# Two projections with streamed activations: weights queued in front of activations

## Reference

```python
# first block, layer 0 (output projection of the mixer)
y_m = head_rmsnorm(h, mnorm_w) * silu(z)              # 1024 columns
y_p = multiscale_pool(u, pool_w, pool_scale) * silu(z2)  # 1024 columns
y   = concatenate([y_m, y_p], -1) @ w_out             # ab_w_out: 2048 x 1024, 1280 rows
x   = x + gate * rmsnorm(y, g_post)
# first block, layer 1: window attention; then the second block's mixers
...
# second block, feed-forward
h = h + conv_ffn(rms_norm(h, norm_ffn), w_up, conv_w, conv_b, w_down)   # w_down: 2816 x 1024
gate = sigmoid(rms_norm(h, norm_ple) @ w_ple_gate)
h = h + gate * (p @ w_ple_proj)
```

## Time and profile before

| | |
|---|---|
| median of 3 runs | 3276.93 us (3276.76 to 3278.3) |
| the profiled execution, its own time | 3276.24 us |
| its span | 3274.5 us |
| mean granted TensorE clock | 0.992 |
| TensorE matmuls busy | 3194.9 us (98%) |
| VectorE busy | 1918.3 us (59%) |
| ScalarE busy | 1615.8 us (49%) |
| out0's matmuls | about 1092 to 1326 us |
| down's matmuls | about 2892 to 3147 us |

### The profile page before, as it was taken

One profiled execution on the slowest core, in us unless ns is written; L12 is line 12 of the kernel. 1 busy time (PEld: TensorE's weight loads), 2 busy tenths in 40 slices (PEclk: granted clock), 3 DMA queues, 4 the chain that ended last, 5 costly groups with the idle time before them and its releaser, 6 DMA issues. The chain is left out here.

```text
span 3274.5 us, 43387 instructions
## 1 busy us (share of the span) xinstructions
PE 3194.9 (98%) x17352; PEld 2616.6 (80%) x17352; DVE 1918.3 (59%) x2974; ACT 1615.8 (49%) x2603; POOL 113.6 (3%) x246
## 2 busy tenths in 40 slices
PE   7999999999999999999999999998999999999998
PEld 5988889898888887888787778886777888878786
DVE  7554444445345468542688454447669888854555
ACT  5343444435333445314788444416646777743455
POOL 2000000000000000001000000000000000000000
PEclk9999999999999999999999999999999999999999
DMA  5202011120533457203400541110162222255564
GB/s 211 69 5 84 30 56 58 42 72 13 174 102 137 181 204 267 87 26 90 104 2 2 154 131 37 46 37 27 46 206 62 80 82 79 71 180 215 210 224 148
DMA packets 198968, 331.49 MB, mean 101 GB/s; under 512 B 28891, under 2 KB 131392, under 8 KB 198640
## 3 DMA queue, kind: packets, MB, share of 16 engines
q1 hardware_dynamic: 176432, 249.23, 23.2%
q0 software_dynamic: 21264, 79.43, 7.0%
q10 hardware_dynamic: 1072, 0.07, 0.0%
HBM read 281.41 MB, written 47.28 MB: 100 GB/s over the span
## 5 line engine op out<-in xcount | busy, mean ns | idle before, releaser
L413 DVE TENSOR_TENSOR W_rounded<-W,W_rounded 128x2048 fp32r<-128x2048 f32 (+2 forms) x184 | 350.6, 1906 | 408.1 <-ACT W_rounded L404 404.2
L2606 PE MATMUL G<-W_rounded,r_y_rounded 128*128 128x512 f32 x2016 | 472.2, 395 | 7.8 <-DVE W_rounded L413 7.5
L404 ACT ACTIVATE W_rounded<-W 128x2048 fp32r<-128x2048 f32 (+1 forms) x172 | 292.8, 1703 | 350.4 <-DMA W<-in_w_down 61.8
L2606 PEld LDWEIGHTS G<-W_rounded,r_y_rounded 128*128 128x128 f32 x2016 | 378.4, 189 | 95.4 <-DVE W_rounded L413 9.5
L1166 PE MATMUL G<-W_rounded,HT_rounded 128*128 128x512 f32 x640 | 213.7, 415 | 0.0
L2231 PE MATMUL G<-HT_rounded,W_rounded 128*128 128x512 f32 (+1 forms) x768 | 207.8, 355 | 0.0
L1210 PE MATMUL G<-HT_rounded,W_rounded 128*128 128x512 f32 (+1 forms) x768 | 206.6, 355 | 1.0 <-PEq L665 1.0
L2954 PE MATMUL G<-W_rounded,HT_rounded 128*128 128x512 f32 x640 | 201.2, 395 | 0.0
L2231 PEld LDWEIGHTS G<-HT_rounded,W_rounded 128*128 128x128 f32 x768 | 136.6, 188 | 24.8 <-issue 3.5
L1210 PEld LDWEIGHTS G<-HT_rounded,W_rounded 128*128 128x128 f32 x768 | 135.8, 188 | 22.4 <-issue 1.2
L2954 PEld LDWEIGHTS G<-W_rounded,HT_rounded 128*128 128x128 f32 x640 | 118.5, 188 | 28.2 <-issue 2.0
(11 more groups left out here) (544 smaller groups left out, 7074.0 us busy)
## 6 DMA issues: line engine op xcount, KB each, us to landing
W<-in_w_down SPq DMA_DIRECT2D x33, 1024.0 KB, 5.4
W<-in_ab_w_out SPq DMA_DIRECT2D x32, 1024.0 KB, 5.8
up_w_in<-in_w_up SPq DMA_DIRECT2D x44, 512.0 KB, 4.4
W<-in_ab_w_in SPq DMA_DIRECT2D x20, 1024.0 KB, 8.7
W<-in_w_mod SPq DMA_DIRECT2D x8, 2048.0 KB, 8.2
x_rows<-r_xt POOLq DMA_DIRECT2D x32, 512.0 KB, 5.5
W<-in_c_w_out SPq DMA_DIRECT2D x24, 512.0 KB, 6.7
r_xt<-x_rows POOLq DMA_DIRECT2D x24, 512.0 KB, 5.1
```

Source lines behind the costliest of these rows:

```text
L404: ins = a.activation(self.half(key, True)[:, at], self.half(key, False, False)[:, at], ACT.Copy)
L413: ins = v.tensor_tensor(self.half(key, False)[:, at], self.half(key, False, False)[:, at], self.half(key, True)[:, at].bitcast(F32), ALU.s ...
L2606: ins = pe.matmul(slot(r)[:, n * 512:(n + 1) * 512], x[y], w[z][:, k, n * 512:(n + 1) * 512], start=(kk == 0 and k == 0 and (y, z) == SPLI ...
```

## The change

In `rows_part` the load of a step's weights, from the fourth step on, moves from behind the activations' transfer to in front of it, and behind the waits. The condition is the same, so the same items are loaded in the same steps. It holds in the streamed projections alone, which are out0 and down.

```diff
@@ -2564,14 +2564,14 @@
                     prev.room(sp, s)
                 if s < per:
                     prev.arrives(sp, kk)
+                if s >= 3 and K.loaded <= K.pl.items[item]:
+                    K.load_item(sp)
                 sp.dma_start(y_part(s, 0, False), stream[:, 2 * kk:2 * kk + 2, rs[0] * P:(rs[-1] + 1) * P])\
                     .then_inc(s_y[s % 3], 16)
                 if s == 2:
                     prev.left(sp)
                     K.load_item(sp)
                     load_gg()
-                    K.load_item(sp)
-                if s >= 3 and K.loaded <= K.pl.items[item]:
                     K.load_item(sp)
         K.load_phase(sp, key, ahead)
         if tail is not None:
```

## The result

In the first comparison the changed kernel took 3282.57 us (median of 14 runs, 3279.12 to 3285.16) against 3277.11 us (14 runs, 3272.12 to 3282.49): ratio 1.0017, 95% interval 1.001 to 1.0024. In a second one, with the same two programs, the ratio was 1.0008, 0.9999 to 1.0017: there the interval just reaches no change at all. So the change costs some 3 to 5.5 us, less than the 0.2% that the prediction named as what can be told. The forecast of 3279.0 had the sign right and the time inside its range. Its difference, 2.1 us, was too small by more than half of the measured one (5.5) in the first comparison, by about a quarter (of 2.8) in the second.

What follows compares the result with a forecast made beforehand. TensorE's matmuls, busy 98% of the span, were taken to bound the kernel. Three waits at 0.65 us (1.95) and 0 to 0.15 from down's last step gave +2.1 on 3276.93: 3279.0 us, range 3276.2 to 3284.5.

Steps and rivals of the forecast that it cites:

- What bounds, and the untouched start of down: TensorE's matmuls bound, busy 98%; down's longest wait, 3.7 us at its start, has loads issued earlier and is not touched.
- The weights land earlier and nobody uses it: In out0 and down weights land about 0.9 us earlier, unused because ScalarE and VectorE still split the activations first.
- The price of a step, 0.65 us: Activations land 5.92 us after the pair's first issue, their split adds 0.52, so the weights' split starts 0.65 us later.
- The prediction's smaller value, 0.52 a step: If the pair's last byte lands at the same time in either order, only the split's 0.52 is left; sum 1.6.
- Three waits without spare time, 3 × 0.65 = 1.95: Two-tile steps where TensorE already waits, 1.08 and 0.39 us in out0, 2.31 in down, pay in full and add up.
- Rival C: Activations behind the weights meet GpSimd's row traffic and pay 2.57 us more a step: sum 9.7, 3286.6 us; chance 0.13.
- In a step with three tiles nothing: Three-tile steps of out0 and down have 5.8 us to spare, so even 1.0 us later costs TensorE nothing.
- the sign that it had named for being wrong: Wrong if pieces land under 4.5 or over 7 us, TensorE waits in three-tile steps, or many two-tile steps wait.
- The rule on arbitration: DMA engines take turns between queues, so row traffic passes beside the weights and activations run alone; sum stays 2.1.
- The sum on record: Total cost of +2.1 us: 1.95 from three waits in out0 and down, 0 to 0.15 from down's last step.

Runs made afterwards that it cites:

- swap, stores first: Changed kernel with GpSimd's queue in out0 and down reordered, a group's stores before the next group's loads: 3276.36 us, ratio 0.9993 against the kernel before.

## Why the prediction was right, and where it was too small

*What bounds, and the untouched start of down.* Right: the start of down waited 3.9 instead of 3.7 us, in the second profile 3.7. TensorE's longest waits outside the two phases are the same as before within some tenths, but for those in the program's first phase.

*The weights land earlier and nobody uses it.* Right, and the experiments show it from both sides: 4.9 us instead of 5.4, no gain in the changed kernel, 2.6 to 2.8 us by the medians once the splits follow the new order.

*The price of a step, 0.65 us.* The mechanism was right, the size too large. The activations were to land 5.92 us after the first issue; in the last step ScalarE started on them at 5.82, over the last five steps of down at 5.6 by the median. The distance of the two splits was 0.54 for 0.52. The weights' split started at 6.36 for 6.44 in the last step, so it paid 0.34 where the text had 0.4 for it. Over the last five steps the median is 6.12 against 5.75 before, 0.37 us a step. So the pair is complete after 5.6 to 5.8 us in either order, and what is paid is the split of the activations less a small gain. The prediction's smaller value, 0.52 a step, was nearer; the Trainium skill, DMA: Bandwidth & Descriptors, section Anatomy of one DMA, from which it has the rule for that value, gives it for transfers issued by GpSimd, and these two are SyncE's.

*Three waits without spare time, 3 × 0.65 = 1.95.* This is the first term that was mis-sized. Down's grew by 0.4 to 0.5. Out0's second wait, 0.39, vanished. The change need not be the reason: in the second profile of the kernel before it is missing too, and with the swap in out0 only there is one of 0.5 behind the 3.4. Out0's first grew by 1.7 and not 0.65. That waits for L413 grew by 1.9 in all (with 0.2 at the start of down) where the sum had 2.1 is luck: none of the three came out at 0.65. In its step the weights' split started 10.46 us after the first issue (1249.33 to 1259.79), before 8.78 (1247.78 to 1256.56), in the step of the first wait of the earlier trace rows. The first two microseconds after the issue, in the changed kernel and before:

```profile
1249.30:1251.30 2.00, 2.00 (x10) 1.62 (x9) 1.97 (x3) 1.50 (x2) 0.93 (x2) 1.00 0.17 39
```

```profile
1247.80:1249.80 2.00, 2.00 (x10) 1.63 (x9) 1.97 (x3) 1.48 (x1) 0.52 (x1) 1.00 0.57 143
```

39 GB/s against 143: GpSimd's load was issued 0.15 us ahead of the pair (1249.18) where it had been 0.5 ahead (1247.26), so less of it had moved when the pair came. An estimate from these rows: 104 GB/s less over 2 us are 208 KB, at the 408 GB/s of the earlier trace rows 0.5 us. With the 0.54 of the split that explains about 1.0 of the 1.68 us; the rest is open. Rival C had named the clash with the rows' traffic, but as activations that pay for it a second time; what these rows show is a later start for all. The lead of GpSimd's load alone doesn't fix the wait: it was 2.2 us with a lead of 0.28 and the old order in all of out0 (swap in down only), and 2.0 with the old order in this step and a lead of 1.0 (swap with three tiles only). It was also 2.3 us with a single transfer of GpSimd's beside the pair (swap, stores first).

*"In a step with three tiles nothing."* This step of the prediction failed, and the sign that it had named for being wrong, a wait of TensorE in steps with three tiles, is there. It counted the spare time of the weights' split, which was enough (5.8 us), and not who else waits on ScalarE: at the end of a group the squares of the second and third finished row stand behind the two splits, and TensorE needs the row's bank. ScalarE behind the splits of out0's tenth step, before and after:

```profile
1158.76 1.01 ACT L2639 ACTIVATE r_sq<-G 128x1024 f32<-128x1024 f32 x1
```

```profile
1160.14 1.01 ACT L2639 ACTIVATE r_sq<-G 128x1024 f32<-128x1024 f32 x1
```

1.4 us later in all, of which 0.5 is a shift that the steps had already, and TensorE waited 0.92 for `r_ty` where it had waited 0.34:

```profile
1163.81 6.57 PE L2606 MATMUL G<-W_rounded,r_y_rounded 128*128 128x512 f32 x27 [0.92 <-DVE r_ty L2694]
```

With the second such wait, 0.42 us near 1234 that wasn't there before, that makes 1.0 us. The version with the swap in three tiles only has the first at 1.0 and no second.

*The clock.* A term that was missing: the wait in out0 had a price beyond its own length, 1.3 us.

*The rule on arbitration.* The Trainium skill, DMA: Bandwidth & Descriptors, section Queues, rings and completion order, spoke against C, since traffic met by the weights would be gone for the activations. In down the trace agrees: there the pair stood beside the same 1 MB of rows, and its wait grew by no more than the split's price. In out0 the wait grew by 1.7, and no run here shows whether the rule held there.

Of the 4.2 us in the profile, then: waits for L413 +1.9 (7.5 to 9.4), for the row's normalisation +1.0, slower matmuls +1.3. The sum on record had the first with 2.1.

## What to carry to other kernels

When two transfers of one step change places on a queue, the order in which their consumers take them has to change too: here each of the two alone cost 0.1 to 0.2%, both together gained 0.1 to 0.2%. Before calling a delay covered, look at everything that stands behind it in program order on the engine that now waits longer, not only at the buffer it fills. And stores that queue behind a load until the tightest steps of a pipeline are worth moving forward: here that alone took away a wait of 2.3 us, and 0.1% of the time.

## What was not expected of the hardware

After a wait of TensorE in out0 the granted clock fell in six profiles (0.91 over 1255 to 1275 in each; in the changed kernel 0.50 right behind the wait, in the one with the swap and the stores first 0.50 over 1266 to 1267, 2.5 us after the matmuls had begun again), with waits of 2.0, 2.0, 2.3, 2.8, 2.9 and 3.4 us, each time with 1.2 to 1.7 us more for the same matmuls. But waits of 2.2 us at the same place (the swap in down only, and the version without swap that splits the weights first) left it at 1.00, and so did those of 2.3 to 3.1 in down. The length of the wait alone doesn't decide it. All six have the swap in steps of out0 and the two at the same place without a fall have not, but what decides isn't settled here.

Out0's wait near 1260 us was 1.1 and 1.2 us in the two profiles of the kernel before and 2.2 where only down's code, far behind it, had changed. Two profiles of one program agreed better (1.1 and 1.2, 2.8 and 2.9, 1.0 and 1.6) than two programs with the same code in this phase. So the difference of one such wait between two programs isn't the effect of an edit to better than a microsecond.
